# An S5, gMLP and expert-mixture inference step: small rows loaded whole, earlier chunk loads, half tables, POOL rotations, eight-row weight runs

## The chip, the cores and the metric

The kernel runs on one NeuronCore of a Trainium2 chip. The core has TensorE (PE, matrix products; its weight loads are listed as PEld), VectorE (DVE), ScalarE (ACT), GpSimd (POOL) and SyncE (SP), which here only issues DMAs. Each engine works through its own instructions in the order in which they were written and waits on semaphores. The metric is the device time of one execution in microseconds; lower is better.

## The reference

One decoder layer over 2048 prompt tokens and 8 sequences of 8 sample tokens, model width 1024. Head group A is a gated MLP that mixes positions within chunks of 128. Head group B is a diagonal complex state-space layer (S5): 32 groups of 16 channels with 64 complex states each, then GELU and GLU. A mixture of 32 experts (top 2) follows.

```python
ada = jax.nn.silu(c) @ w_ada + b_ada
h = modulate(x, g_norm1, sh1, sc1)
proj = h @ w_in                      # 1024 -> 3 x 512
u = jax.nn.gelu(proj[..., :D_A]); v = head_layer_norm(gelu(proj[..., D_A:2 * D_A]), ln_g, ln_b)
s_in = proj[..., 2 * D_A:]
a_out = u * chunk_spatial_mix(v, w_s, b_s)
# S5: h_t = (ar + i ai) h_{t-1} + (br + i bi) u_t, ar + i ai = exp((lam_re + i lam_im) exp(log_dt))
y = C_re h_re - C_im h_im + d_skip * u
b_out = gelu(y) * sigmoid(gelu(y) @ w_glu + b_glu)
x = x + gt1 * (jnp.concatenate([a_out, b_out]) @ w_out)
h = modulate(x, g_norm2, sh2, sc2)
x = x + gt2 * hier_moe(h, ...)       # h = silu(xb @ w1[e]) * (xb @ w3[e]); h @ w2[e]
```

Outputs are the final normed rows, the S5 states and the sample rows of v. All is float32; a product is made of three matmuls on high and low parts ("hi" and "lo").

## The kernel before

Five stages follow each other, each a block of its own with one written program per engine: `front` (L283), `s5` (L1186), `mixout` (L1517), `route` and `experts` (L1922, L2175) and `final`. In the trace the front lies from 0 to 488 us, the recurrence (`s5`) to 688, mixout to about 1045, the expert stage from 1107 to about 1620.

The front takes the 17 token tiles in six groups of three or two (`FRONT`). Group 0 is special: SP loads the vectors and w_ada (L446 to L475), PE makes the modulation row (L755), DVE adds its bias (L980), and w_in is loaded in 12 pieces by POOL and split into high and low parts by ACT (`win_s` and `uv`) and DVE (`low_piece`). For each group PE computes the s part, then v, then u (`rows_step`); before each u step it turns a piece of the next group's x (L773), which ACT copies with the gain and DVE splits (`low`, L963). DVE has, beside that, to build the S5 tables: `powers`, `factors`, `rotations` (18 complex products, L1022 to L1037, `cmul` at L905 to L909) and for each of 16 pairs of groups `pair(p)` (L1039 on), of which POOL stores 1536 columns as `s5_tables` (L593 to L604) and the toeplitz rows. DVE runs `rotations()` between two u steps of group 0. POOL, after the w_in pieces, stores the sample blocks of w_s (L577), then rows of the bias (L580), then a zero pad for the toeplitz rows (L587); DVE's first pair waits for the pad.

The recurrence works on chunks of 8 tokens. SP loads in a written order (L1246 on): 16 chunk rows, 8 sample groups of 64-byte pieces, two tables, the initial states, 8 toeplitz loads, then two more tables; in each batch of two pairs it loads the next two tables as soon as both outputs are computed, and stores y. ACT and DVE regroup the chunk rows by group of channels, PE turns them (`fill`) into uT. Then for a batch b, PE runs `additions(b + 2)` (the terms that enter the states, L1349), DVE the scan over chunks (`batch(b)`, ends with L1479), and PE the two `outputs` (L1365 to L1372). In between DVE makes the low parts of w_glu and w_out (`low(n)`, L1446).

```python
                for b in range(NBATCH):
                    outputs(2 * b)
                    outputs(2 * b + 1)
                    if b + 2 < NBATCH:
                        additions(b + 2)
```

Mixout loads y (12 DMAs for the first group, L1607), multiplies with the GLU weight (L1685), waits with the sigmoid `z` (L1774) for `small_ld`, which counts the router's small loads too, and adds the output product (L1708 to L1710). Meanwhile POOL writes zeros over the blocks of `expert_rows` that may stay empty (L1668), eight of them at once and the others as tiles are done. The expert stage gathers rows (xg), turns them by 128 columns (L2342), splits them, and multiplies with the weights of each expert; `hid` is turned at L2374.

## Time and profile before

| | us |
|---|---|
| median of 3 runs | 1751.36 (1748.81 to 1752.66) |
| the profiled execution | 1746.57 |
| its span on the core | 1744.8 |
| granted TensorE clock, mean | 0.869 of 2.4 GHz |

| engine | busy us | share | instructions |
|---|---|---|---|
| PE | 1323.8 | 76% | 6756 |
| PEld | 1051.4 | 60% | 6757 |
| DVE | 960.4 | 55% | 2307 |
| ACT | 588.1 | 34% | 979 |
| POOL | 392.1 | 22% | 400 |

The page also divides the span into 40 slices of 43.6 us. A digit is the busy share in tenths:

```profile
PE   1686999998926663399899982799999999999100
DVE  1368646656324342154466658586555476565398
PEclk9698999999966776699999985599999999999655
DMA  5634354351277543655446210799877599795686
```

The slices 12 to 16 are the recurrence, slice 24 is the routing. DMAs moved 338.55 MB. A DMA share can exceed 1 in the windows.

### The profile page before, as it was taken

The page shows a single profiled execution, that of the slowest core. Times are in us where ns is not written, and L with a number is a line of the kernel's source. Part 1 is how long each engine was busy: PE and PEld are TensorE (multiplying, and loading weights), DVE is VectorE, ACT ScalarE, POOL GpSimd, SP SyncE. Part 2 cuts the span into 40 slices and gives each one's busy share as a digit, 9 for nine tenths or more (in the row PEclk, how much of TensorE's full clock was granted, in tenths as well). Part 3 has the DMA queues.
Part 4 walks back from the last instruction along what each step waited for, and adds up shares of the span by engine and source line. Part 5 has one row for each costly group of instructions (what it writes and reads, how often), then busy time and mean ns, then how long its engine had stood idle before and what let it go on. Part 6 is the DMA issues. An engine that isn't in the chain of part 4 may idle for free. (4 is left out here: it accounts for less than half of the span.)

```text
span 1744.8 us, 25676 instructions
## 1 busy us (share of the span) xinstructions
PE 1323.8 (76%) x6756; PEld 1051.4 (60%) x6757; DVE 960.4 (55%) x2307; ACT 588.1 (34%) x979; POOL 392.1 (22%) x400
## 2 busy tenths in 40 slices
PE   1686999998926663399899982799999999999100
PEld 0464777776725552378788871587778877778000
DVE  1368646656324342154466658586555476565398
ACT  2352425233211111121122110276545476565111
POOL 0011202112100001000010000256442356364331
PEclk9698999999966776699999985599999999999655
DMA  5634354351277543655446210799877599795686
GB/s 190 203 101 124 107 175 165 123 164 57 71 193 151 156 146 81 188 159 161 157 156 194 103 61 29 248 311 382 312 248 252 181 358 388 266 363 199 250 327 258
DMA packets 184993, 338.55 MB, mean 194 GB/s; under 512 B 31545, under 2 KB 119689, under 8 KB 183890
## 3 DMA queue, kind: packets, MB, share of 16 engines
q1 hardware_dynamic: 159538, 250.92, 43.5%
q0 software_dynamic: 25376, 86.66, 14.8%
q8 instruction: 40, 0.66, 0.2%
q14 instruction: 39, 0.32, 0.1%
HBM read 242.98 MB, written 94.40 MB: 193 GB/s over the span
## 5 line engine op out<-in xcount | busy, mean ns | idle before, releaser
L2312 POOL TENSOR_TENSOR down_lo<-expert_raw,down_hi (+1 forms) x64 | 153.5, 2420 | 201.5 <-ACT down_hi L2406 201.5
L2456 DVE TENSOR_TENSOR up_lo<-expert_raw,up_hi (+1 forms) x128 | 160.7, 1315 | 19.2 <-ACT up_hi L2401 16.4
L256 PE MATMUL ps_up<-up_hi,xT_hi 128*128 x400 | 162.0, 405 | 6.1 <-DVE up_lo L2456 2.9
L257 PE MATMUL ps_up<-up_lo,xT_hi 128*128 x400 | 157.2, 393 | 0.0
L258 PE MATMUL ps_up<-up_hi,xT_lo 128*128 x400 | 156.9, 392 | 0.0
L2401 ACT ACTIVATE up_hi<-expert_raw (+1 forms) x128 | 125.3, 1060 | 1.6 <-issue 0.5
L1708 PE MATMUL ps_out<-wout_hi,catT 128*128 128x512 f32 (+1 forms) x272 | 108.4, 399 | 0.0
L1710 PE MATMUL ps_out<-wout_hi,catT 128*128 128x512 f32 (+1 forms) x272 | 106.8, 393 | 0.0
L1709 PE MATMUL ps_out<-wout_lo,catT 128*128 128x512 f32 (+1 forms) x272 | 106.8, 392 | 0.0
L256 PEld LDWEIGHTS ps_up<-up_hi,xT_hi 128*128 128x128 f32 x400 | 75.8, 189 | 26.3 <-issue 11.9
L258 PEld LDWEIGHTS ps_up<-up_hi,xT_lo 128*128 128x128 f32 x400 | 75.8, 189 | 16.4
L257 PEld LDWEIGHTS ps_up<-up_lo,xT_hi 128*128 128x128 f32 x400 | 75.9, 190 | 14.3
L1668 POOL DMA_DIRECT2D expert_rows<-blank x31 | 26.8, 986 | 250.2 <-DVE x L1857 245.8
L2394 ACT ACTIVATE xT_hi<-ps_xT 128x512 fp32r<-128x512 f32 x102 | 55.4, 599 | 70.1 <-PE ps_xT L2342 69.5
L2450 DVE TENSOR_TENSOR xT_lo<-ps_xT,xT_hi 128x512 fp32r<-128x512 f32 x102 | 65.7, 686 | 22.3 <-ACT xT_hi L2394 21.8
L258 PE MATMUL ps_y<-down_hi,hidT_lo 128*128 x196 | 77.6, 396 | 0.0
L256 PE MATMUL ps_y<-down_hi,hidT_hi 128*128 x196 | 77.5, 396 | 0.0
L257 PE MATMUL ps_y<-down_lo,hidT_hi 128*128 x196 | 77.5, 396 | 0.0
L2406 ACT ACTIVATE down_hi<-expert_raw (+1 forms) x64 | 64.3, 1053 | 32.6 <-issue 28.1
L2306 POOL DMA_INDIRECT xg<-moe_in_rows,idx x54 | 59.4, 1100 | 43.2 <-POOL idx L2303 42.4
L2473 DVE TENSOR_SCALAR yo<-ps_y,gcol 128x512 f32<-128x512 f32 x49 | 36.7, 748 | 55.3 <-PE ps_y L258 54.1
L1795 ACT ACTIVATE h<-x 128x1024 f32<-128x1024 f32 (+1 forms) x17 | 18.0, 1061 | 144.5 <-DVE x L1857 144.5
(407 smaller groups left out, 3115.2 us busy)
## 6 DMA issues: line engine op xcount, KB each, us to landing
expert_raw<-in_w SPq DMA_DIRECT2D x96, 1024.0 KB
expert_rows<-yo SPq DMA_DIRECT2D x49, 512.0 KB
x<-in_x_prompt SPq DMA_DIRECT2D x32, 512.0 KB, 4.8
stage<-in_w_ada SPq DMA_DIRECT2D x32, 512.0 KB, 4.3
expert_rows<-blank POOLq DMA_DIRECT2D x31, 512.0 KB, 5.6
tab<-s_tables SPq DMA_DIRECT2D x16, 768.0 KB, 5.4
wada_early<-in_w_ada SPq DMA_DIRECT2D x8, 1024.0 KB, 15.4
s_tables<-pair_scratch POOLq DMA_DIRECT2D x32, 256.0 KB, 2.6
```

The costliest lines, as they stand in the source:

```text
L256: pe.matmul(out, left(0, k), right(0, k), start=k == 0, stop=False)
L257: pe.matmul(out, left(0, k), right(1, k), start=False, stop=False)
L258: last = pe.matmul(out, left(1, k), right(0, k), start=False, stop=k == n - 1)
L1708: pe.matmul(out, cat[:, 0, k, spot(m)], S.wout_hi[:, k, cols], start=k == 0, stop=False)
L1709: pe.matmul(out, cat[:, 0, k, spot(m)], S.wout_lo[:, k, cols], start=False, stop=False)
L1710: last = pe.matmul(out, cat[:, 1, k, spot(m)], S.wout_hi[:, k, cols], start=False, stop=k == KD - 1)
L2306: pool.indirect_dma_start(out=xg[:, par, :], out_offset=None, in_=S.h2_d, in_offset=bass.IndirectOffsetOnAxis(ap=idx[:, par:par + 1], axis ...
L2312: pool.tensor_tensor(down_piece(down_lo, run, m), raw_piece(run, 2, m, 1), down_piece(down_hi, run, m).bitcast(F32), ALU.subtract).then_in ...
L2401: act.activation(up_piece(up_hi, run, m), raw_piece(run, m // 2, m % 2, KD // 2), ACT.Copy).then_inc(up_h, 1)
L2406: act.activation(down_piece(down_hi, run, m), raw_piece(run, 2, m, 1), ACT.Copy).then_inc(down_h, 1)
L2450: dve.tensor_tensor(xT_lo[:, par, ks, :], pX[:, h, :].rearrange("p (k t) -> p k t", k=4), xT_hi[:, par, ks, :].bitcast(F32), ALU.subtract) ...
L2456: dve.tensor_tensor(up_piece(up_lo, run, m), raw_piece(run, m // 2, m % 2, KD // 2), up_piece(up_hi, run, m).bitcast(F32), ALU.subtract).t ...
```

## The change

1. In the front's start, `dt`, the first norm's gain and the gMLP bias are each loaded as whole rows, and the last two are turned by PE beside the lambdas. In the SBUF plan, `win_s` moves ahead of the early w_ada area.
2. The 18 complex products of the rotations run on POOL with a tile set of their own; DVE's pair 0 waits for them before it uses the rotations.
3. The chunk rows are loaded by SP in the front's last group and regrouped there (first half of the channels) by ACT.
4. In the recurrence a table comes as two halves, one that the additions and the scan need (`state_tables`) and one for the outputs (`output_tables`). The sample rows are one load, regrouped by POOL and ACT. The router's small loads are issued there. POOL makes the low parts of the weights. Additions stand between the two outputs of a batch.
5. In mixout, half of the first y loads are issued by ACT, and every blank block waits for a finished tile.
6. Expert weights are read with 8 (w1, w3) or 2 (w2) neighbouring rows per partition, and xg and hid are turned by columns that lie 8 or 2 apart.

```diff
-        ldt = a.log_dt[0:1, :].rearrange("o (a g) -> o g a", g=2)
-        for g in range(2):
-            sp.dma_start(dt[g * ST:(g + 1) * ST, :], ldt[:, g, :].to_broadcast([ST, PAIRS])).then_inc(lam_ld, 16)
+        sp.dma_start(dt[:, :], a.log_dt[0:1, :].to_broadcast([P, G])).then_inc(lam_ld, 16)
+        sp.dma_start(g1row, a.g_norm1.rearrange("o (k p) -> (o k) p", p=P)).then_inc(lam_ld, 16)
+        sp.dma_start(bsrow, a.b_s[0]).then_inc(lam_ld, 16)
...
-                sp.dma_start(g1col[:, :], a.g_norm1.rearrange("o (k p) -> p (o k)", p=P)).then_inc(brow_ld, 16)
...
+        sp.wait_ge(s_out, 16 * NT)
+        sp.wait_ge(s_mm, NT)
+        rows = S.s_d[0:SEQ, :].rearrange("(c s) n -> s c n", s=Q)
+        for kt in range(2):
+            for m in range(8):
+                sp.dma_start(S.chunk[:, 8 * kt + m, :], rows[8 * kt + 7 - m]).then_inc(S.chunk_ld[kt], 16)
...
+        def tmul(o_re, o_im, x_re, x_im, y_re, y_im, t):
+            turns.did(pool.tensor_tensor(o_re, x_re, y_re, ALU.mult))
+            turns.did(pool.tensor_tensor(o_im, x_re, y_im, ALU.mult))
+            turns.link(pool.tensor_tensor(t, x_im, y_im, ALU.mult))
+            turns.link(pool.tensor_tensor(o_re, o_re, t, ALU.subtract))
+            turns.link(pool.tensor_tensor(t, x_im, y_re, ALU.mult))
+            turns.link(pool.tensor_tensor(o_im, o_im, t, ALU.add))
+
+        def rotations():
+            own = [t[:, :] for t in turn_c]
+            (cr, ci), (er, ei) = (tmp[5][:, :], tmp[3][:, :]), own[0:2]
+            spare = own[2:4]
+            pool.wait_ge(pw_ok, 1)
+            for i in range(4):
+                tmul(er, ei, cr, ci, cr, ci, own[4])
+                (cr, ci), (er, ei) = (er, ei), spare if i == 0 else (cr, ci)
+            for t, top in ((rB, 16), (rA, 8)):
+                turns.did(pool.memset(t[:, 0, :, 0:1], 1.0))
+                turns.link(pool.memset(t[:, 1, :, 0:1], 0.0))
+                n = 1
+                while n < top:
+                    sh = [P, PAIRS, n]
+                    tmul(t[:, 0, :, n:2 * n], t[:, 1, :, n:2 * n], t[:, 0, :, 0:n], t[:, 1, :, 0:n], fan(cr, sh), fan(ci, sh),
+                         turn_t[:, :, 0:n])
+                    tmul(er, ei, cr, ci, cr, ci, own[4])
+                    (cr, ci), (er, ei) = (er, ei), (cr, ci)
+                    n *= 2
+            pool.sem_inc(turn_ok, 1)
...
+        rotations()
...
+            if g == NF - 1:
+                act.wait_ge(v_mm, NT)
+                for kt in range(2):
+                    act.wait_ge(S.chunk_ld[kt], 16 * 8)
+                    act.activation(*by_group(S, kt, 0), ACT.Copy).then_inc(S.grouped_a, 1)
...
+            if p == 0:
+                dve.wait_ge(turn_ok, 1)
...
+        def load_tx(p):
+            sp.dma_start(tx[:, p % NB, :], S.tab_d[p][:, 0:HALF]).then_inc(tx_ld[p % NB], 16)
+
+        def load_ty(p):
+            sp.dma_start(ty[:, p % NB, :], S.tab_d[p][:, HALF:TABW]).then_inc(ty_ld[p % NB], 16)
+
+        sp.dma_start(work[0:NSEQ, 0:DSEQ * DA].rearrange("q (t n) -> q t n", t=DSEQ),
+                     S.s_d[SEQ:TOK, :].rearrange("(q t) n -> q t n", t=DSEQ)).then_inc(ss_ld, 16)
         for i, t in enumerate((a.state_ssm_re, a.state_ssm_im)):
             sp.dma_start(h0_in[:, i, :], t[0].rearrange("q (a g) p -> (q a) (g p)", g=2)).then_inc(h0_ld, 16)
+        for p in range(NB):
+            load_tx(p)
         for m in range(8):
             s = 7 - m
             sp.dma_start(toep[m * GC:(m + 1) * GC, :, :], S.kpad_d[:, :, P - s * GC:2 * P - s * GC]).then_inc(toep_ld, 16)
-        for p in range(2, 4):
-            load_tab(p)
+        for p in range(NB):
+            load_ty(p)
+        sp.dma_start(S.bglu[:, :], a.b_glu.rearrange("o (j p) -> p (o j)", p=P)).then_inc(S.small_ld, 16)
+        sp.dma_start(S.wr[:, :, 0:EG], a.w_group[0].rearrange("(k p) n -> p k n", p=P)).then_inc(S.small_ld, 16)
+        sp.dma_start(S.wr[:, :, EG:NR], a.w_expert[0].rearrange("(k p) n -> p k n", p=P)).then_inc(S.small_ld, 16)
+        sp.dma_start(S.br[:, 0:EG], a.b_group.to_broadcast([P, EG])).then_inc(S.small_ld, 16)
+        sp.dma_start(S.br[:, EG:NR], a.b_expert.to_broadcast([P, NE])).then_inc(S.small_ld, 16)
...
+            if 2 * b + NB < PAIRS:
+                sp.wait_ge(h_ok, 2 * b + 2)
+                for p in (2 * b, 2 * b + 1):
+                    load_tx(p + NB)
+                for p in (2 * b, 2 * b + 1):
+                    sp.wait_ge(y_mm, 2 * p + 2)
+                    load_ty(p + NB)
...
+        pool.tensor_copy(*samples(0)).then_inc(ss_ok, 1)
         for n in range(10):
-            if n >= 2:
-                pool.wait_ge(w_l, n - 1)
-            pool.dma_start(raw_part(n), part(w_glu, w_out, n)).then_inc(raw_ld[n % 2], 16)
+            pool.wait_ge(w_h, n + 1)
+            pool.tensor_tensor(part(S.wglu_lo, S.wout_lo, n), raw_part(n), part(S.wglu_hi, S.wout_hi, n).bitcast(F32),
+                               ALU.subtract).then_inc(w_l, 1)
+            if n + 2 < 10:
+                pool.wait_ge(w_l, n + 1)
+                load(n + 2)
...
         for b in range(NBATCH):
             outputs(2 * b)
-            outputs(2 * b + 1)
             if b + 2 < NBATCH:
                 additions(b + 2)
-
-        pe.wait_ge(fin_ok, 2)
-        pe.wait_ge(x_free, NBATCH)
-        for i in range(2):
-            pe.transpose(pX[0:PAIRS, 0, 0, i * P:(i + 1) * P], h[:, :, i, CH], ident[:, :])
-        for i in range(2):
-            last = pe.transpose(pX[:, 1, 0, i * P:(i + 1) * P], fin[:, i, :, :].rearrange("p q a -> p (q a)"), ident[:, :])
-        last.then_inc(f_mm, 1)
+            if b == NBATCH - 1:
+                finals()
+            outputs(2 * b + 1)
...
-            if n >= FULL + 8:
-                pool.wait_ge(x2_ok, (n - FULL - 8) // 2 + 1)
+            pool.wait_ge(x2_ok, (n - FULL) // 2 + 1)
...
+        for n, i in enumerate(GROUPS[0]):
+            for k in range(2, 4):
+                act.dma_start(yf[:, k, n * P:(n + 1) * P], y_rows(i, k)).then_inc(y_ld2, 16)
+        act.wait_ge(y_ld2, 32 * len(GROUPS[0]))
...
-    return [(t[0].rearrange("e (k p) n -> e p k n", p=P), k) for t, k in ((a.w1, KD), (a.w3, KD), (a.w2, DE // P))]
+    return [(t[0].rearrange("e (p k) n -> e p k n", p=P), k) for t, k in ((a.w1, KD), (a.w3, KD), (a.w2, DE // P))]
...
-                last = pe.transpose(pX[:, k // 4, k % 4 * P:(k % 4 + 1) * P], xg[:, q, k * P:(k + 1) * P], ident[:, :])
+                last = pe.transpose(pX[:, k // 4, k % 4 * P:(k % 4 + 1) * P], xg[:, q, :].rearrange("p (c k) -> p k c", k=KD)[:, k, :], ident[:, :])
...
-                last = pe.transpose(pT[:, k * P:(k + 1) * P], hid[:, k * P:(k + 1) * P], ident[:, :])
+                last = pe.transpose(pT[:, k * P:(k + 1) * P], hid[:, :].rearrange("p (c k) -> p k c", k=KH)[:, k, :], ident[:, :])
```

**Where instructions stand.** SP in the recurrence's start before (`tab` is a whole table; L1248 the chunk rows):

```order
L1248 DMA chunk_rows<-s_in 128x512 x16
L1256 DMA sample_groups<-s_in 8x32x16 x8
L1253 DMA tab<-s_tables 128x1536 x2
L1261 DMA h_in<-in_state_ssm_re 128x128
L1261 DMA h_in<-in_state_ssm_im 128x128
L1264 DMA toep<-toeplitz_rows 16x32x128 x8
L1253 DMA tab<-s_tables 128x1536 x4
L1273 DMA s_out<-ys 128x4x128 x2
```

and now (`wr`, `bglu`, `br` are the router's and the GLU's small loads):

```order
L1300 DMA s_work<-s_in 8x4096
L1303 DMA h_in<-in_state_ssm_re 128x128
L1303 DMA h_in<-in_state_ssm_im 128x128
L1295 DMA state_tables<-s_tables 128x768 x4
L1308 DMA toep<-toeplitz_rows 16x32x128 x8
L1298 DMA output_tables<-s_tables 128x768 x4
L1311 DMA bglu<-in_b_glu 128x4x1
L1312 DMA wr<-in_w_group 128x8x4
L1313 DMA wr<-in_w_expert 128x8x32
L1314 DMA br<-in_b_group 128x4
L1315 DMA br<-in_b_expert 128x32
L1295 DMA state_tables<-s_tables 128x768 x2
```

The chunk rows left for the front, and the small loads stand ahead of the first tables that are loaded again. POOL in the front, after the w_in pieces, before (`spatial_bias_sample` is the bias rows, `toeplitz_rows` the zero pad):

```order
L577 DMA ws_samp<-ws 8x4x8 x8
L580 DMA spatial_bias_sample<-spatial_bias 8x512 x8
L586 MEMSET pair_scratch 16x128
L587 DMA toeplitz_rows<-pair_scratch 512x1x128
L588 TENSOR_TENSOR pair_scratch<-ident,dd 16x512
```

and now, with the start and the end of the rotations (18 products of six instructions, and four MEMSETs):

```order
L627 DMA ws_samp<-ws 8x4x8 x8
L590 TENSOR_TENSOR turn_c<-tmp 128x16
L591 TENSOR_TENSOR turn_c<-tmp 128x16
L592 TENSOR_TENSOR turn_c<-tmp 128x16
L593 TENSOR_TENSOR turn_c<-turn_c 128x16
L594 TENSOR_TENSOR turn_c<-tmp 128x16
...
L595 TENSOR_TENSOR turn_c<-turn_c 128x16
L631 DMA spatial_bias_sample<-spatial_bias 8x512 x8
L637 MEMSET pair_scratch 16x128
L638 DMA toeplitz_rows<-pair_scratch 512x1x128
```

The bias rows and the pad now stand behind the rotations. PE in a batch of the recurrence, before (`ps_s` are outputs, `ps_state` additions):

```order
L1372 MATMUL ps_s<-h,tab 128x128 x4
L1365 MATMUL ps_s<-uT,toep 128x136 x2
L1372 MATMUL ps_s<-h,tab 128x136 x4
...
L1372 MATMUL ps_s<-h,tab 128x128 x4
L1349 MATMUL ps_state<-uT,tab 64x136 x2
L1349 MATMUL ps_state<-uT,tab 64x128 x2
```

and now:

```order
L1435 MATMUL ps_s<-h,output_tables 128x128 x4
L1411 MATMUL ps_state<-uT,state_tables 64x136 x2
L1411 MATMUL ps_state<-uT,state_tables 64x128 x2
...
L1411 MATMUL ps_state<-uT,state_tables 64x128 x2
L1428 MATMUL ps_s<-uT,toep 128x136 x2
L1435 MATMUL ps_s<-h,output_tables 128x136 x4
```

The additions moved from behind the second output of a batch to between the two.

## Rows read from the trace of the kernel before

**Rows 1.** Windows: stretch, length; PE, PEld, DVE, ACT, POOL busy; clock; DMA share; GB/s

```profile
5.00:25.00 20.00, 0.32 (x3) 0.22 (x3) 0.23 (x1) 0.48 (x1) 0.00 (x0) 1.00 0.17 47
25.00:55.00 30.00, 13.27 (x62) 1.88 (x66) 8.75 (x34) 8.41 (x15) 1.45 (x2) 0.74 1.00 381
520.00:535.00 15.00, 10.09 (x100) 9.62 (x100) 8.23 (x16) 5.21 (x10) 1.11 (x2) 0.84 1.28 114
545.00:678.00 133.00, 84.23 (x642) 69.12 (x640) 49.29 (x133) 18.64 (x45) 3.19 (x6) 0.74 0.40 123
1150.00:1600.00 450.00, 436.66 (x2084) 352.24 (x2083) 277.76 (x389) 276.89 (x402) 217.58 (x148) 1.00 0.86 304
```

**Rows 2.** Timeline of the start: begin, length, engine, line, operation, [idle before]

```profile
26.70 0.22 ACT L615 ACTIVATE tmp<-dt 128x16 f32<-128x16 f32 x1 [21.22 <-DMA dt<-in_log_dt]
57.93 0.68 DVE L980 TENSOR_TENSOR u<-ps_a,u 128x512 f32<-128x512 f32 x1
```

**Rows 3.** Timeline 100 to 206 us; then one wait, DMA and group row

```profile
105.45 4.41 POOL L577 DMA_DIRECT2D ws_samp<-ws  x8 [0.29 <-POOL ws L571]
...
152.69 1.09 PE L896 MATMUL ps_x<-ident,pair_scratch 128*128 128x128 f32 x4 [14.64 <-ACT rs_col L730]
...
169.78 0.42 DVE L1061 TENSOR_TENSOR pair_scratch<-pw_re,bb 128x256 f32<-128x256 f32 x1
...
198.13 0.49 PE L773 MATMUL ps_t<-ident,x 128*128 128x128 f32 x3
...
200.82 0.55 DVE L963 TENSOR_TENSOR hT<-h,hT 128x384 fp32r<-128x384 f32 x1
...
201.42 0.49 PE L773 MATMUL ps_t<-ident,x 128*128 128x128 f32 x3
...
203.56 0.32 POOL L601 TENSOR_TENSOR pair_scratch<-pair_scratch 16x32 f32<-16x32 f32 x1 [5.81 <-ACT pair_scratch L672]
...
DVE stats L1098 <- ACT v L680: 12.3, 3, 4.5
...
toeplitz_rows<-pair_scratch POOLq DMA_DIRECT2D x1, 256.0 KB, 6.0
...
L2303 POOL COPY idx<-slot_tok 128x1 int32 (+1 forms) x54 | 33.1, 613 | 72.6 <-POOLq L1977 61.0 <-PE ps_xT L2342 10.7 <-issue 0.5
```

**Rows 4.** Timeline of the recurrence

```profile
502.54 1.91 ACT L1408 ACTIVATE chunk_groups<-chunk_rows 128x2048 f32<-128x2048 f32 x1 [21.86 <-DMA chunk_rows<-s_in]
...
559.99 2.03 PE L1349 MATMUL ps_state<-uT,tab 128*64 128x136 f32 x16 [3.69 <-DMA tab<-s_tables]
...
581.38 1.28 PE L1365 MATMUL ps_s<-uT,toep 128*128 128x136 f32 x4 [1.84 <-DVE h L1479]
...
650.49 1.28 PE L1365 MATMUL ps_s<-uT,toep 128*128 128x136 f32 x4 [1.79 <-DVE h L1479]
...
676.96 0.71 PE L1372 MATMUL ps_s<-h,tab 64*128 64x128 f32 x8
```

**Rows 5.** Timeline of the way into mixout

```profile
688.27 17.65 SPq L1607 DMA_DIRECT2D yf<-s_out  x12
...
711.47 1.77 ACT L1763 ACTIVATE yT<-yf 128x384 fp32r<-128x384 f32 x4 [31.86 <-DMA yf<-s_out]
...
726.44 1.05 ACT L1774 ACTIVATE z<-ps_z,bglu 128x384 f32<-128x384 f32 x2 [8.38 <-DMA br<-in_b_expert]
...
738.45 0.48 PE L1708 MATMUL ps_out<-wout_hi,catT 128*128 128x512 f32 x1
```

**Rows 6.** Weight loads by form: least, median, largest ns; last, mean ns

```profile
L2342 PEld LDWEIGHTS ps_xT<-ident,xg x408: 138/141/230, 1113.3 to 1609.5; 128*128 128x128 f32 x136
...
L1390 PEld LDWEIGHTS ps_state<-ident,h x2: 93/98/103, 682.9 to 683.0; 128*16 128x16 f32 x2
...
L1392 PEld LDWEIGHTS ps_state<-ident,fin x2: 226/226/226, 683.1 to 683.3; 128*128 128x128 f32 x2
...
L755 PEld LDWEIGHTS ps_a<-wada_early,cT 128*32 128x32 f32 x64 | 1.6, 136 | 26.0 <-DMA wada_early<-in_w_ada 23.7 <-DVE tmp L928 2.2
```

More of the change, by code:

```diff
@@ L190, in build @@
         S.blocks_out, S.pad_out = (ctx.enter_context(nc.semaphore(n)) for n in ("ws_blocks", "pad_stored"))
+        S.chunk_ld = [ctx.enter_context(nc.semaphore(f"chunk_loaded{i}")) for i in range(2)]
+        S.grouped_a, S.small_ld = (ctx.enter_context(nc.semaphore(n)) for n in ("groups_act", "router_loaded"))
+        S.logits = sb(ctx, "logits", [P, NT, NR])
+        with ExitStack() as start:
+            S.chunk = sb(start, "chunk_rows", [P, Q, DA])
+            S.turn = sb(start, "chunk_groups", [P, 2, G, 8 * GC])
         names, used = ExitStack(), []
@@ L195, in build @@
         assert [t.num for t in used] == list(S.spent)
-        S.logits = sb(ctx, "logits", [P, NT, NR])
         with ExitStack() as mid:
-            with ExitStack() as start:
-                S.turn = sb(start, "chunk_groups", [P, 2, G, 8 * GC])
             S.wout_hi = sb(mid, "wout_hi", [P, KD, D], F32R)
-            with ExitStack() as start:
-                S.chunk = sb(start, "chunk_rows", [P, Q, DA])
             S.wout_lo = sb(mid, "wout_lo", [P, KD, D], F32R)
@@ L275, in first_token, with by_group @@
     return GROUPS[g][0] * P
+def by_group(S, kt, half):
+    gs = slice(half * G // 2, (half + 1) * G // 2)
+    src = S.chunk[:, 8 * kt:8 * kt + 8, half * DA // 2:(half + 1) * DA // 2].rearrange("p m (g o) -> p g m o", o=GC)
+    return S.turn[:, kt, gs, :].rearrange("p g (m o) -> p g m o", o=GC), src
 FRONT = ((0, 1, 2), (3, 4, 5), (6, 7, 8), (9, 10, 11), (12, 13, 14), (15, TP))
@@ L287, in front @@
         W = TPG * P
+        win_s = sb(st, "win_s", [P, 2, KD, DA], F32R)
         with ExitStack() as early:
@@ L327, in front @@
         li = sb(st, "li", [P, PAIRS])
-        dt = sb(st, "dt", [P, PAIRS])
+        dt = sb(st, "dt", [P, G])
+        turn_c = [sb(st, f"turn_c{i}", [P, PAIRS]) for i in range(5)]
+        turn_t = sb(st, "turn_tmp", [P, PAIRS, 8])
         tmp = [sb(st, f"tmp{i}", [P, PAIRS]) for i in range(8)]
@@ L613, in _ @@
                 st_.did(act.activation(c9, c9, ACT.Silu))
-                act.wait_ge(lam_ld, 64)
-                st_.link(act.activation(tmp[7][:, :], dt[:, :], ACT.Exp))
+                act.wait_ge(lam_ld, 80)
+                by_pair = dt[:, :].rearrange("p (a g) -> p g a", g=2)
+                act.activation(tmp[7][0:ST, :], by_pair[0:ST, 0, :], ACT.Exp)
+                st_.link(act.activation(tmp[7][ST:P, :], by_pair[ST:P, 1, :], ACT.Exp))
                 act.wait_ge(dv, 2)
@@ L919, in _ @@
                 c.did(dve.tensor_copy(lr[:, :], pT[:, 0:PAIRS]))
+                c.did(dve.tensor_copy(g1col[:, :], pT[:, 2 * PAIRS:2 * PAIRS + KD]))
+                c.did(dve.tensor_copy(bs_col[:, :], pT[:, 2 * PAIRS + KD:2 * PAIRS + KD + HEADS]))
                 c.link(dve.tensor_copy(li[:, :], pT[:, PAIRS:2 * PAIRS]))
@@ L1168, in _ @@
                             factors()
-                        if g == 0 and k == 4:
-                            rotations()
                         if k < 5 or g == NF - 1:
@@ L1207, in s5 @@
         ident = S.ident
-        c_ld = [sem(f"chunk_loaded{i}") for i in range(2)]
-        p_a, p_d, ss_ld, f_mm0, e_a, e_d, ys_ok, ys_out = (sem(n) for n in (
-            "groups_act", "groups_dve", "sample_loaded", "turned_mm", "uT_copied_act", "uT_copied_dve", "y_sample_copied", "y_sample_stored"))
-        tab_ld = [sem(f"tables_loaded{i}") for i in range(NB)]
+        p_d, ss_ld, ss_ok, f_mm0, e_a, e_d, ys_ok, ys_out = (sem(n) for n in (
+            "groups_dve", "sample_loaded", "sample_grouped", "turned_mm", "uT_copied_act", "uT_copied_dve", "y_sample_copied",
+            "y_sample_stored"))
+        tx_ld, ty_ld = ([sem(f"{n}_tables_loaded{i}") for i in range(NB)] for n in ("state", "output"))
         raw_ld = S.weights_ld
@@ L1228, in raw_part, with samples @@
             return raw[:, n % 2, :].rearrange("p (k n) -> p k n", k=2) if n < 2 else raw[:, n % 2, :]
-        def by_group(kt, half):
+        def samples(half):
             gs = slice(half * G // 2, (half + 1) * G // 2)
-            src = S.chunk[:, 8 * kt:8 * kt + 8, half * DA // 2:(half + 1) * DA // 2].rearrange("p m (g o) -> p g m o", o=GC)
-            return S.turn[:, kt, gs, :].rearrange("p g (m o) -> p g m o", o=GC), src
+            src = srow[:, ::-1, gs, :].rearrange("q t g h -> q g t h")
+            return S.samp[:, gs, :].rearrange("q g (m h) -> q g m h", m=DSEQ), src
         def evacuated(n):
@@ L1370, in outputs @@
                                 r = slice(g * ST, (g + 1) * ST)
[L1371 to L1372 removed]
+                                m0 = 256 + 256 * i + 128 * half
+                                last = pe.matmul(pY[:, banks[g], at:at + width], ty[r, p % NB, m0:m0 + P], h[r, p, i, lo:CH],
                                                  start=False, stop=i == 1)
@@ L1438, in _ @@
                         hi(b + 2)
+                act.wait_ge(ys_ok, NBATCH)
+                for m in range(8):
+                    act.dma_start(S.ys_d.rearrange("(g o) t q -> t o g q", o=GC)[m], ysamp[m * GC:(m + 1) * GC, :, :]).then_inc(ys_out, 16)
             @block.vector
@@ L1600, in load_y @@
                     for n, i in enumerate(GROUPS[g]):
-                        for k in range(4):
+                        for k in range(4 if g else 2):
                             if i == TP:
```

188 lines of the change are left out of this document (80 added, 108 removed).

## The prediction

> **What bounds the kernel now.** I read four views in this order. The first page's busy digits in 40 slices show that TensorE (PE) works nearly all the time in three long stages (front, mixout, experts) and that holes lie at the start, near 150 us, in the recurrence and between recurrence and mixout. The windows put numbers on the holes [rows 1]: 0.32 us of PE work in the 20 us from 5, 84 of 133 us in the recurrence. The experts are full (437 of 450 us), so only something that lengthens PE's own work can matter there. The timelines then show what ends each hole: transfers at the start [rows 2], VectorE (DVE) near 150 [rows 3], transfers and DVE in turn in the recurrence [rows 4], transfers again into mixout [rows 5]. Last, rows by form give the price of a weight load [rows 6]. The profiled execution took 1746.57 us; the runs' median is 4.8 us above it. I sum against the former and carry the gain over unchanged.
>
> **Start: small rows loaded whole: -17.** From 5 to 25 us the core moved 47 GB/s at a DMA share of 0.17, and 381 GB/s from 25 to 55 [rows 1]: the queues were behind pieces of 4 bytes. dt, two broadcasts of 64 x 16 such pieces (2048), was awaited for 21.22 us by the Exp at 26.70 [rows 2]; g1col adds 1024 and bs_col 512. All become rows of 128 to 512 bytes. The eight w_ada pieces (8.4 MB), x (1.6), the bias rows (0.3) and the first w_in pieces (about 2.1) are some 12 MB, at the later rate 32 us; from 4 us on that is about 36 us. The gate for all that follows is DVE's add at 57.93, behind w_ada and a w_in piece; that piece I put at 39 and the add at 41: 17 us earlier. Everything up to the recurrence hangs on this add. Bounds: 14 (a third of the old stall stays) to 20 (the whole low stretch).
>
> **Rotations from DVE to GpSimd (POOL): -12.** PE waited 14.64 us until 152.69, while DVE computed 18 complex products [rows 3]; a hole also leaves a low clock behind it (the mean is 0.74 in the recurrence's window, 1.00 in the experts'), which I estimate at 2 us here: 16.6 gross. POOL has no row for this shape. Nearest: 0.32 us for 16x32, and 0.29 us of waiting after another POOL instruction (at 105.45). A product is six instructions with four such hops: 6 x 0.32 + 4 x 0.29 = 3.1, times 18 = 56 us. The bounds are 44 (two hops hidden) and 92 (0.61 us a small instruction, as in the mean of POOL's idx copies, plus hops). POOL starts at 110 in the old count, ends at 166, issues eight DMAs (4.4 us, as the eight at 105.45) and the pad store, which lands 6.0 later: 177. DVE's pair(0) waits for that store; it would otherwise start at 169.78 - 16.6 = 153. After it DVE owes, before the first low of the next group's hT, its work between 169.78 and 200.82: 31.0 less waits of 12.3 = 18.7. So that low comes at 195.7, against 200.82 - 16.6 = 184.2. PE can work two turns ahead (3.3 us each, 198.13 to 201.42), so of these 11.5 it stands about 4.6. Net -12. Up to some 51 us on POOL nothing stands; at 92 the stall is 40 and the edit costs 21: bounds -16.6 and +21, my value lies by the nearest row. That the pair tables come later I price at nothing: PE's steps in the front don't wait for them, and the last of them is stored well within the groups that follow.
>
> The Trainium skill ("SBUF — State Buffer", section "SBUF: two separate sides") has POOL and DVE lock one shared port pair when DVE reads two SBUF inputs. The rotations then delay DVE's two-input work and it them. No row here has this pairing at this size; by the rule POOL's 56 us would grow by the share of DVE's busy time, towards 75, the stall with it.
>
> **Chunk rows in the last group: +0.6.** ACT groups its halves before the last group's GELUs, 2 x 1.91 us less its idle time there. In exchange the recurrence starts without this load.
>
> **Recurrence: -36.** (a) Its first work waited for chunk rows until 502.54 [rows 4]; loaded early, PE can start 15 us sooner. (b) But what then gates is the tables. The eight toeplitz loads are 4096 pieces of 512 bytes, 2.1 MB at the 114 GB/s seen then [rows 1]: 18.5 us, done about 517.5; four output tables, 522.5; then five small router loads, some 2800 pieces of 4 to 16 bytes. Before, with 2304 such pieces in the queue behind y, their reader went at 726.44, 15 us after y's at 711.47 [rows 5]; so about 14 us here, since they start at an empty queue, and the state tables for batch 2, queued behind them, land near 542. additions(2), at 559.99 before after a wait for its tables, begins about 543: -17. (c) Periods were (650.49 - 581.38)/4 = 17.3 us, with PE waiting 1.8 for DVE's h in each. The table of the next batch no longer waits for both outputs, DVE no longer splits weights, and additions stand between the two outputs: I take 15.5 (13 if only PE's work of 84/133 of the time remains plus one hop; 17 if DVE's scan still sets it): -7 over four. (d) At the end the two last batches (the last outputs began at 676.96, 26.5 after the row at 650.49) need about 8 each: -10. (e) The ys stores leave SP: -2. Together -36, bounds 22 (tables at 556, period 17) and 52 (at 533, 13). The ten splits go to POOL, busy for 3.2 of 133 us there; without that cover, mixout's first product would wait for the last.
>
> **Into mixout: -27.5.** Before, y landed at 711.47, 23 us after the stage began: twelve loads by SP beside 4 MB of blank rows. Then ACT's z waited 8.38 more, until 726.44, for the router's small loads [rows 5]; project(0) began at 738.45. Now the loads are shared by two engines, no blanks run beside, and the small ones are done. y after about 6.5 us, the GLU in the 12 us from 726.44 to 738.45, 4 us of turning and copying before: 22.7 after the stage's start at 688.3 where it was 50.2. Bounds 20 and 30. The blanks go to later stages, where POOL idles; 4 MB at 381 GB/s are 11 us of a queue that is used to 0.4 to 0.9, and cost nothing as long as PE is not waiting for transfers.
>
> **Experts: -1.** Weights come in runs of 8 KB in place of 1 to 4 KB, at 304 GB/s and a share of 0.86; but PE idles only 13 of 450 us, so little can be had. The price is that 408 transposes of xg read columns 32 bytes apart and 100 of hid 8 bytes apart. The load of xg takes 141 ns now [rows 6]. A load of 16 columns from h at a stride of over 1 KB took 98 ns; by contiguous ones of 32 columns (136) and 128 (226 at the low clock) 16 columns would take about 121. So a stride shows no price here. Bounds: -3 and +35 (below).
>
> **Sum.** -17 - 12 + 0.6 - 36 - 27.5 - 1 = -93: the profile at 1653.6, the median at 1658.
>
> **The rivals.**
> B: the recurrence stays gated and the rotations are long. For it: DVE's scan ended PE's wait each period; POOL's price is not measured. Recurrence -22, rotations -2: gain about 68, time 1684.
> C: the queue clears fast. If the small loads are spread over the 16 engines beside the tables, these land at 533, the period is 13, and the shorter holes leave the clock high (0.74 in the recurrence's window, 1.00 in the experts'). Start 20, rotations 15, recurrence 48, mixout 30: gain 117, time 1634. Against it: the 15 us behind the old small loads.
> D: the strided weight load runs at half its rate. Then 141 ns become the low clock's 226: +85 ns on 408 loads, +35: 1693. If the load reads the wrong side of the pair (moving), the same price falls on the 98 ns row, which does not show it.
> The Trainium skill ("SBUF — State Buffer", "Specifications (TRN2)") says that a 16-byte line wants at least two hits for full bandwidth; xg at 32 bytes has one per line. That speaks against the change; the row of h disagrees with it, at 16 columns only.
> E, the other side: the same mechanism, far dearer. PE is full in this stage, so nothing hides it: from 93/408 = 0.23 us more per transpose the whole gain is gone, and at 0.25 the time is about 1760. That is nearly three times the present load.
>
> **How the numbers follow.** A result within 0.2% of before (3.5 us, about what the runs can tell apart) would need several of these to cancel. Chances: the forecast 0.50 (1640 to 1680), C 0.17, B 0.15, D 0.12, E and anything like it 0.06. The range 1626 to 1700 takes in B, C and most of D. Faster 0.93, same 0.02, slower 0.05.
>
> **What would show it.** Start: no wait for dt, DVE's first add near 41 us. Rotations: POOL busy for about 35 of 56 us in a run of L590 to L595 rows, and a PE wait before group 1's u steps of about 5 us; none means that POOL was faster. Recurrence: the first PE wait for state tables near 540, behind the small loads' landing; if it ends before 535, C. Mixout: project(0) about 23 us after the stage's first y load. Experts: the load for ps_xT at 141 ns; over 200 means D or E. The forecast is wrong if the recurrence and the way into mixout together give under 45 us or over 85.

## The result, and the profile after

| | before | after |
|---|---|---|
| median of 4 runs, us | 1750.09 | 1634.01 (1632.02 to 1638.78) |
| ratio to before | | 0.935 (0.9333 to 0.9368) |
| span of the profiled execution, us | 1744.8 | 1630.3 |
| granted TensorE clock, mean | 0.869 | 0.892 |

The forecast was 1658, with its own range from 1640 to 1680 and 1626 to 1700 in all; what came lies 24 us below it, at the time that rival C had. The gain of 116 us divides by stage as follows (times in us from the start of the span). Each line takes an event of both traces; the differences are between one execution of each, and in the kernels here that share its front PE's first turn of the recurrence begins between 453.65 and 456.23 us. The additions of batch 2 (`additions`, the terms that enter the states) ran in two halves before, at 555.18 and 559.99; the row takes the second, as the prediction did, and from the first the step would be 4.8 us less.

| event | before | after | moved | this step | forecast |
|---|---|---|---|---|---|
| DVE's first add (u from ps_a) | 57.93 | 39.54 | -18.4 | -18.4 | -17 |
| SP's first load of the recurrence | 489.94 | 456.52 | -33.4 | -15.0 | -11.4 |
| additions of batch 2 | 559.99 | 500.29 | -59.7 | -26.3 | -17 |
| last output's products | 676.96 | 590.73 | -86.2 | -26.5 | -17 |
| first y load of mixout | 688.27 | 600.20 | -88.1 | -1.8 | -2 |
| first product of project(0) | 738.45 | 626.93 | -111.5 | -23.4 | -27.5 |
| first turn of xg | 1113.33 | 1004.01 | -109.3 | +2.2 | 0 |
| last turn of hid | 1618.04 | 1504.86 | -113.2 | -3.9 | -1 |
| end of the span | 1744.8 | 1630.3 | -114.5 | -1.3 | 0 |

Windows of the start, after, with the columns of [rows 1]: the quiet 20 us are gone, and the 30 us after them are no longer full.

```profile
5.00:25.00 20.00, 8.65 (x40) 1.56 (x39) 5.42 (x33) 8.19 (x16) 0.00 (x0) 1.00 0.99 398
25.00:55.00 30.00, 15.53 (x63) 6.65 (x64) 11.15 (x19) 11.23 (x18) 2.89 (x4) 0.70 0.52 187
```

The timeline of the start, after, answers [rows 2]: dt's reader at 7.85, not 26.70, and the add at 39.54.

```profile
7.85 0.21 ACT L668 ACTIVATE tmp<-dt 64x16 f32<-64x16 f32 x1
...
39.54 0.68 DVE L1043 TENSOR_TENSOR u<-ps_a,u 128x512 f32<-128x512 f32 x1
```

The timeline of the rotations, after, answers [rows 3]: the first product on POOL, the last instruction, the DMAs behind it, and DVE's wait.

```profile
90.16 0.23 POOL L590 TENSOR_TENSOR turn_c<-tmp 128x16 f32<-128x16 f32 x1
90.33 0.23 POOL L591 TENSOR_TENSOR turn_c<-tmp 128x16 f32<-128x16 f32 x1
90.51 0.22 POOL L592 TENSOR_TENSOR turn_c<-tmp 128x16 f32<-128x16 f32 x1
90.81 0.22 POOL L593 TENSOR_TENSOR turn_c<-turn_c 128x16 f32<-128x16 f32 x1
91.11 0.22 POOL L594 TENSOR_TENSOR turn_c<-tmp 128x16 f32<-128x16 f32 x1
91.41 0.24 POOL L595 TENSOR_TENSOR turn_c<-turn_c 128x16 f32<-128x16 f32 x1
91.73 0.22 POOL L590 TENSOR_TENSOR turn_c<-turn_c 128x16 f32<-128x16 f32 x1
...
128.16 0.22 POOL L595 TENSOR_TENSOR turn_c<-turn_c 128x16 f32<-128x16 f32 x1
129.03 4.60 POOL L631 DMA_DIRECT2D spatial_bias_sample<-spatial_bias  x8 [0.65 <-POOL turn_c L595]
...
139.45 0.43 DVE L1107 TENSOR_TENSOR pair_scratch<-pw_re,bb 128x256 f32<-128x256 f32 x1 [5.25 <-DMA toeplitz_rows<-pair_scratch]
```

A product of 16 columns takes 1.57 us (90.16 to 91.73), not 3.1; those that fill the tables have up to 128 columns, and all 18 take 38 us, not 56. DVE waits 5.25 us for the pad. PE's only wait between 100 and 200 us is 0.88 us, for a weight of the modulation; the old one of 14.64 is gone.

PE's three longest waits from 440 to 640 us, after (us in total, times, longest). The first two are the recurrence's, the third is mixout's:

```profile
PE ps_state L1411 <- DMA state_tables<-s_tables: 25.2, 6, 5.2
PE ps_s L1428 <- DMA output_tables<-s_tables: 14.8, 1, 14.8
PE ps_aT L1746 <- DMA a_rows<-gmlp_rows: 11.5, 1, 11.5
```

From batch 2 on the additions wait 3.6 to 5.2 us for their state tables in each batch. One period of the recurrence's timeline, after, shows why (it answers the rows at 581.38 and 650.49 of [rows 4]):

```profile
514.40 3.43 PE L1411 MATMUL ps_state<-uT,state_tables 128*64 128x136 f32 x32 [3.95 <-DMA state_tables<-s_tables]
517.76 0.94 PE L1428 MATMUL ps_s<-uT,toep 128*128 128x136 f32 x4
...
521.15 0.32 SPq L1298 DMA_DIRECT2D output_tables<-s_tables  x1
521.85 0.92 SPq L1322 DMA_DIRECT2D s_out<-s_work  x2
...
522.82 1.20 SPq L1295 DMA_DIRECT2D state_tables<-s_tables  x2
523.12 2.40 POOL L1357 TENSOR_TENSOR wout_lo<-weights_raw,wout_hi 128x1024 fp32r<-128x1024 f32 x1 [10.51 <-ACT wout_hi L1465]
523.36 2.45 DVE L1538 TENSOR_TENSOR h<-s_work 128x256 f32<-128x256 f32 x1
...
528.20 3.57 PE L1411 MATMUL ps_state<-uT,state_tables 128*64 128x136 f32 x32 [4.03 <-DMA state_tables<-s_tables]
```

SP issues the next state tables at 522.82, behind a load of output tables at 521.15 and its store of y at 521.85. The load waits for the second outputs and the store for their GELU, and PE runs the second outputs behind the additions of 514.40. From 528.20 back: 5.4 us of landing, 1 us of stores, 0.7 of GELU, 3.4 of outputs, 3.4 of additions. It is a circle of 13.8 us through the order in which SP and PE were written. The store and its GELU are about 1.7 us of it; without them the wait for the second outputs, at the output tables, would hold the next state tables all the same. A second thing stands out: DVE's subtraction takes 2.45 us beside POOL's split, where the same instruction took 0.42 before the change.

### The profile page after: what moved, and what is told of

It is laid out like the page before. It is cut to its first block and busy times, and to the rows that moved or that the text cites. A ratio compares the mean times of both kernels' runs of the same rounds, so it can differ in the third digit from the quotient of the medians.

```text
span 1630.3 us, 25699 instructions
## 1 busy us (share of the span) xinstructions
PE 1313.5 (81%) x6758; PEld 1046.3 (64%) x6759; DVE 942.7 (58%) x2187; ACT 589.4 (36%) x981; POOL 452.2 (28%) x523
```

## The experiments

Each changes one thing in the changed kernel, the later ones in its successor as told. The kernel before was run on the same chip each time, its medians between 1746.8 and 1749.9; a difference in us is that of the ratios times 1750, against 0.935. The changed kernel's own interval is 3 us to each side, so a difference under about 5 us is not told apart from none: this holds for low_dve, small_in_mixout, plain_turns and old_layout. Those of chunk_in_s5 and blanks_now are just clear of it.

| kernel | median | ratio (95%) | against the changed one, us |
|---|---|---|---|
| sp_order | 1600.99 | 0.9153 (0.9137 to 0.9169) | -34 |
| low_dve | 1634.89 | 0.9358 (0.9334 to 0.9382) | +1 |
| sp_order_low_dve | 1611.22 | 0.9210 (0.9195 to 0.9226) | -25 |
| pe_order | 1596.67 | 0.9137 (0.9119 to 0.9155) | -37 |
| rot_dve | 1650.62 | 0.9432 (0.9416 to 0.9447) | +14 |
| dt_pieces | 1652.30 | 0.9444 (0.9428 to 0.9459) | +16 |
| chunk_in_s5 | 1641.49 | 0.9382 (0.9357 to 0.9406) | +6 |
| small_in_mixout | 1639.27 | 0.9368 (0.9353 to 0.9384) | +3 |
| blanks_now | 1642.04 | 0.9391 (0.9366 to 0.9416) | +7 |
| plain_turns | 1631.98 | 0.9345 (0.9322 to 0.9368) | -1 |
| old_layout | 1632.88 | 0.9351 (0.9312 to 0.9391) | 0 |
| toep_two_queues | 1597.98 | 0.9140 (0.9118 to 0.9162) | -37 |

**sp_order.** SP issues the next state tables ahead of the output tables and the store.

```diff
-                for b in range(NBATCH):
+                def next_tx(b):
                     if 2 * b + NB < PAIRS:
                         sp.wait_ge(h_ok, 2 * b + 2)
                         for p in (2 * b, 2 * b + 1):
                             load_tx(p + NB)
+
+                next_tx(0)
+                for b in range(NBATCH):
+                    next_tx(b + 1)
+                    if 2 * b + NB < PAIRS:
                         for p in (2 * b, 2 * b + 1):
                             sp.wait_ge(y_mm, 2 * p + 2)
...
```

> Changed kernel, but SP issues the state tables of batch b+3 ahead of the output tables of batch b+2 and of the y store of batch b. Theory loop: the 14.4 us from one additions to the next are a circle through SP's written order (additions 3.4, second outputs 3.3, GELU and y store about 2, then the table is issued and lands 5.4 later). With the table issued at h, the period falls to PE's own work, 10 to 11 us, and 5 periods give 17 to 22 us: about 1614 us. Rival scan: h itself is late (DVE's last subtraction takes 2.45 us beside POOL's split), the issue moves little, and the time stays above 1626 us.

The gain is larger than either theory had it. PE's timeline in sp_order:

```profile
503.00 3.51 PE L1416 MATMUL ps_state<-uT,state_tables 128*64 128x136 f32 x32 [3.50 <-DMA state_tables<-s_tables]
512.56 2.02 PE L1416 MATMUL ps_state<-uT,state_tables 128*64 128x136 f32 x32
520.63 2.02 PE L1416 MATMUL ps_state<-uT,state_tables 128*64 128x136 f32 x32
```

The period is 8.07 us (512.56 to 520.63), not 10 to 11. I had added PE's work from rows behind a wait, at the low clock. The windows of one additions each, first two of the changed kernel and then one of sp_order, with the columns of [rows 1] (the granted clock is the number ahead of the DMA share; 0.50 is 1.2 GHz, 1.00 is 2.4):

```profile
500.30:504.00 3.70, 3.70 (x32) 3.37 (x32) 0.00 (x0) 0.00 (x0) 0.00 (x0) 0.50 0.27 107
514.40:517.76 3.36, 3.35 (x32) 3.03 (x32) 0.00 (x0) 0.00 (x0) 0.00 (x0) 0.56 0.63 253
...
512.56:514.58 2.02, 2.02 (x35) 1.85 (x33) 2.02 (x2) 0.67 (x2) 1.72 (x2) 1.00 0.69 206
```

The additions take 2.8 to 3.8 us behind their waits, at granted clocks of 0.50 to 0.71, and 2.02 us at 1.00 once PE has no holes. The waits cost twice, by themselves and by the clock.

**low_dve.** The splits on DVE, one behind each batch; POOL only loads.

```diff
-                    pool.tensor_tensor(part(S.wglu_lo, S.wout_lo, n), raw_part(n), ...)
+                    dve.tensor_tensor(part(S.wglu_lo, S.wout_lo, n), raw_part(n), ...)   # low(n), behind batch(n - 1)
```

> Changed kernel, but DVE makes the low parts of w_glu and w_out in the recurrence (one after each batch) and POOL only loads. Theory loop: DVE is not in the circle; the 128x256 subtraction falls from 2.45 to about 0.42 us, but additions start when they did: 1631 to 1636 us. Rival scan: h 2 us earlier in each of 8 batches, less 1.2 for the split when it is in the way: 1620 to 1626 us.

The time is 1634.89, in the theory's range: DVE is not in the circle. The subtraction is short there (0.42 us in all eight batches), and the last additions still begin at 572.08, against 572.15 in the changed kernel.

**sp_order_low_dve.** Both. 

> Both edits together. Theory loop: PE's own work is the bound once the table is early, so this is within 3 us of the kernel with SP's order alone, 1610 to 1617 us. Rival scan: only here, with h early and the table early, does the period fall; 8 us or more below the better of the two single edits.

Neither theory: it is 10 us slower than sp_order alone. The median lies in the first range, 1610 to 1617, but that range stood around a sp_order of 1614, so this is luck. Once PE is the bound, DVE's order matters again: PE waits for h three times, up to 3.25 us (at 562.51), where in sp_order it never does after its first outputs. The row of the split, by line (busy, mean ns, idle before it):

```profile
L1566 DVE TENSOR_TENSOR wout_lo<-weights_raw,wout_hi 128x1024 fp32r<-128x1024 f32 x8 | 9.8, 1225 | 42.3 <-ACT wout_hi L1466 42.3
```

The split waits 42.3 us in all for ACT, and the next batch's scan stands behind it (how much of the 42.3 DVE would have idled anyway is not shown). POOL is the better place here, in spite of the collision.

**pe_order.** PE's old order in the recurrence.

```diff
                     outputs(2 * b)
-                    if b + 2 < NBATCH:
-                        additions(b + 2)
                     if b == NBATCH - 1:
                         finals()
                     outputs(2 * b + 1)
+                    if b + 2 < NBATCH:
+                        additions(b + 2)
```

> Changed kernel, but PE computes both outputs of a batch and then the additions of batch b+2, as before the change. Theory loop: the store of y no longer stands behind the additions, the table lands beside the second outputs, period 10 to 11 us: about 1614 us, as with SP's order; so putting the additions in the middle cost what the half tables could have given. Rival, as in my forecast: the additions in the middle keep DVE fed, and taking them back costs 1 to 2 us a period: 1642 to 1650 us.

The circle opens from the other side, with the same result and a little more: the additions of batch 2 (499.48) have no wait either, where sp_order's waited 3.50. The forecast of this run, 1614, had the same error as sp_order's, PE's work at the low clock. A window over five periods, PE, PEld, DVE, ACT, POOL busy as in [rows 1]:

```profile
499.00:540.00 41.00, 40.98 (x450) 34.92 (x452) 30.92 (x89) 12.61 (x30) 14.56 (x10) 1.00 0.96 317
```

PE is full at the full clock. So additions between the outputs, which I had counted as a gain, cost 37 us with SP's order as it is. No kernel here is faster than this one, 9% below the one before.

**rot_dve.** The 18 products back on DVE between two u steps of group 0.

```diff
+                        if g == 0 and k == 4:
+                            turn_on_dve()       # as rotations() before
...
-                rotations()                     # on POOL
...
-                    if p == 0:
-                        dve.wait_ge(turn_ok, 1)
```

> Changed kernel with the 18 products of the rotations back on DVE, between two u steps of group 0. Theory: on POOL they cost nothing (PE has no wait there, DVE's pad wait of 5.2 us hides), so all of the old hole comes back: 1649 to 1652 us, with a PE wait of about 14.6 us. Rival: other work had shrunk that hole by now, under 8 us come back: below 1642 us.

All of it comes back (1650.62, in the theory's range), with the old hole in PE's timeline:

```profile
133.16 1.09 PE L955 MATMUL ps_x<-ident,pair_scratch 128*128 128x128 f32 x4 [14.61 <-ACT rs_col L782]
```

**dt_pieces.** Only dt in 4-byte pieces again.

```diff
-                sp.dma_start(dt[:, :], a.log_dt[0:1, :].to_broadcast([P, G])).then_inc(lam_ld, 16)
+                for g in range(2):
+                    sp.dma_start(dt[g * ST:(g + 1) * ST, 0:PAIRS], ldt[:, g, :].to_broadcast([ST, PAIRS])).then_inc(lam_ld, 16)
```

> Changed kernel, but dt is loaded again as two broadcasts of 64x16 pieces of 4 bytes (2048 pieces); the gain and bias rows stay whole. Theory: dt's pieces at the head of the queues made the quiet 20 us, so 14 to 18 of the 18.4 us come back: 1648 to 1652 us. Rival: g1col's 1024 pieces did as much, in proportion 2048 of 3584: about 10 us, 1644 us.

These 2048 pieces alone bring back the whole stall. The windows of its start, and its add:

```profile
5.00:25.00 20.00, 0.52 (x5) 0.42 (x4) 0.23 (x1) 0.68 (x1) 0.00 (x0) 1.00 0.16 44
25.00:55.00 30.00, 13.56 (x64) 2.09 (x68) 8.89 (x36) 8.38 (x15) 1.44 (x2) 0.69 0.99 380
...
58.02 0.68 DVE L1043 TENSOR_TENSOR u<-ps_a,u 128x512 f32<-128x512 f32 x1
```

58.02 against 57.93 before: g1col in pieces had cost nothing that shows here. SP issued it only at 28.23 us, behind the quiet stretch, and bs_col later still.

**chunk_in_s5.** The 16 chunk loads and ACT's grouping at the recurrence's start. 

> Changed kernel with the chunk rows loaded and grouped by ACT at the recurrence's start, as before. Theory queue: the first outputs wait for toeplitz and output tables, whose 512-byte pieces hold the queue; the 16 loads in front push these by 9 us and PE's fill has slack of 15 us, so about 9 to 12 us are lost: 1643 to 1646 us. Rival: the full 15 us of the fill's start are lost, 1649 us or more.

PE's first turns begin 15.3 us later, its first outputs 11.3 later, and these wait for h, no longer for tables. The last additions are 9.7 us later (581.86 against 572.15), as the theory had it. By the ratios about 6 us are lost (1 to 10), and the median is a little under its range:

```profile
471.53 3.67 PE L1375 MATMUL ps_state<-ident,chunk_groups 128*128 128x128 f32 x16 [23.10 <-ACT chunk_groups L1469]
...
502.38 1.24 PE L1423 MATMUL ps_s<-uT,toep 128*128 128x136 f32 x4 [7.27 <-DVE h L1537]
```

**small_in_mixout.** The five small loads behind the first y loads again. 

> Changed kernel with the router's five small loads back in mixout, behind the first y loads. Theory: in the recurrence they cost little (3.6 us wait for tables at 500 us), and in mixout z waits for them as before (8.4 us and the low clock after it): net 5 to 8 us slower, 1639 to 1642 us. Rival of my forecast: they hold the first state tables by 12 us or more in the recurrence, so moving them out gains there what it costs later: 1630 to 1636 us.

```profile
602.48 1.76 ACT L1813 ACTIVATE yT<-yf 128x384 fp32r<-128x384 f32 x4 [16.13 <-DMA yf<-s_out]
...
617.31 1.05 ACT L1824 ACTIVATE z<-ps_z,bglu 128x384 f32<-128x384 f32 x2 [8.61 <-DMA br<-in_b_expert]
```

The old wait returns in z (8.61 us), and the recurrence gives part of it back: its last additions begin 111.5 us behind its first turn (453.65 to 565.13), 4.4 less than in the changed kernel (456.23 to 572.15). By the ratios 3 us stay, by the medians 5; the theory's range has the one and not the other.

**blanks_now.** Eight blank blocks written at mixout's start. 

> Changed kernel, but POOL writes eight blank blocks (4 MB) at mixout's start, as before. Theory: they share the transfers with y, which lands 5 us or more later than its 9.7 us: 1639 to 1644 us. Rival: y was late for SP's issue of twelve loads, which two engines now share, and the blanks only fill free time: 1632 to 1637 us.

The theory holds, 1642.04 in its range: y's first reader waits 28.20 us, 11.7 more than the 16.48 of the changed kernel, so the blanks don't only fill free time:

```profile
621.82 1.76 ACT L1815 ACTIVATE yT<-yf 128x384 fp32r<-128x384 f32 x4 [28.20 <-DMA yf<-s_out]
```

**plain_turns** reads xg and hid by contiguous columns; **old_layout** has the old weight layout as well.

```diff
-    xg[:, q, :].rearrange("p (c k) -> p k c", k=KD)[:, k, :]
+    xg[:, q, k * P:(k + 1) * P]
...
-    hid[:, :].rearrange("p (c k) -> p k c", k=KH)[:, k, :]
+    hid[:, k * P:(k + 1) * P]
```

> Changed kernel with contiguous columns in the turns of xg and hid, the weight layout kept (so the experts' result is not the reference's). Theory: the strided weight load is slower (193 against 141 ns) but runs beside the moving columns: eight turns take 1.06 us against 1.04, so at most 1 to 2 us are gained: 1632 to 1634 us. Rival: 52 ns on 508 loads are exposed, 26 us gained: 1608 us.

> Changed kernel with the weights' old layout (runs of 4 and 1 KB) and contiguous turns. Theory: the longer runs gave 3 to 5 us in the experts' stage (its first to last turn 492.4 us against 496.2), so 1636 to 1639 us. Rival: the layout did nothing, that difference is chance: 1632 to 1635 us, as with plain turns.

The turns' loads by form (least, median, largest ns), changed kernel:

```profile
L2397 PEld LDWEIGHTS ps_xT<-ident,xg x408: 185/193/231, 1004.0 to 1496.4; 128*128 128x128 f32 x136
```

plain turns:

```profile
L2397 PEld LDWEIGHTS ps_xT<-ident,xg x408: 137/141/230, 1001.1 to 1493.2; 128*128 128x128 f32 x136
```

The stride does have a price, 52 ns a load, but the 408 matmuls beside it are busy for 57.6 us with it and 55.6 without: 2 us are exposed, and 1.7 on the 100 turns of hid (21.7 against 20.0). The layout's gain is not settled by the runs: old_layout's median, 1632.88, lies in the rival's range, with an interval of 7 us to each side. The traces say more. The span from the first xg turn to the last hid turn is 504.7 us before and 503.6 in old_layout, 500.9 after and 500.6 in plain_turns, and between 500.5 and 502.8 in the ten other kernels, which all have the new layout: about 3 us for the longer runs.

**toep_two_queues** is pe_order, with four of the eight toeplitz loads issued by ACT. 

> The kernel with PE's old order in the recurrence, and ACT issues four of the eight toeplitz loads. Theory queue: the loads of 512-byte pieces are held by one engine's queue (SP's issue of eight takes 16 us), two queues run side by side, and the first outputs start 5 to 8 us earlier: 1589 to 1592 us. Rival transfers: the pieces themselves fill the transfer engines (share 1.28 in that window before), so nothing is gained, and ACT's copies come later by the issue: 1596 to 1602 us.

The wait for output tables falls from 16.7 to 8.1 us, but PE's earlier work is pushed back by the ACT queue's issue and by h_in, which lands later, so the first outputs gain 2.7 us (488.11 against 490.79); the additions of batch 2 then wait 3.52 for tables and start at 499.51, where pe_order has 499.48:

```profile
465.44 0.69 PE L1387 MATMUL ps_s<-ident,h_in 128*128 128x128 f32 x2 [4.12 <-DMA h_in<-in_state_ssm_im]
...
488.11 1.24 PE L1428 MATMUL ps_s<-uT,toep 128*128 128x136 f32 x4 [8.12 <-DMA output_tables<-s_tables]
499.51 3.79 PE L1411 MATMUL ps_state<-uT,state_tables 128*64 128x136 f32 x32 [3.52 <-DMA state_tables<-s_tables]
```

The rival's range holds. From 459 us to the first outputs the DMA share is 1.12 to 1.13 in pe_order and 1.13 to 1.17 here, and SP's four toeplitz issues take 13.88 us where eight took 15.98: the second queue adds little where the transfers are full, and what is gained at one wait is lost at the next.

## Why the prediction was right, and where its sizes were off

The range held and the order of the gates held; the middle was 24 us too high, most of it in the recurrence. That the time is rival C's to the microsecond is luck: C's own terms (20, 15, 48 and 30) add up to 113 and not 117, so its time should have been 1638, and its parts came otherwise: 18.4, 15.0, 54.6 and 23.4. By the prediction's sign, recurrence and way into mixout between 45 and 85 us, they gave 78.

**Start (-17, was -18.4).** Right in mechanism and size. The pieces of dt were the whole of it, shown by dt_pieces; that g1col and bs_col shared the blame, as the text counted their pieces, falls.

**Rotations and last group (-11.4, were -15.0).** The gross gain of 16.6 was right (rot_dve, +14 by the ratio and 16.6 by the medians, with PE's wait of 14.61). The mis-sized term is POOL's price: 56 us forecast, 38 measured. I took a row of 0.32 us and added a full hop of 0.29 behind each dependent instruction; the trace has 0.22 us and 0.30 from start to start of dependent ones. At 38 us POOL stays under the 51 from which PE would stand, as the working itself said. (Two slips in it: 11.5 less two turns of 3.3 us is 4.9, not 4.6, and at 92 us of POOL the edit would have cost about 24, not 21.) The stretch to 75 us did not come, but the collision behind it is in the trace, one instruction at a time: a POOL instruction whose like takes 0.22 us took 1.26 beside one of DVE with two SBUF inputs.

```profile
93.97 1.22 DVE L1007 TENSOR_TENSOR uv<-stage,uv 128x1024 fp32r<-128x1024 f32 x1
94.01 1.26 POOL L593 TENSOR_TENSOR turn_c<-turn_c 128x16 f32<-128x16 f32 x1
```

About 18 of the 112 instructions are longer than their like, the others of them at 0.38 to 0.80 us. Taken from the shortest distance between the same two instructions, an estimate is 7 of the 38 us; that each of them met DVE is not shown.

**Recurrence up to batch 2 (-17, was -26.3).** The order of gates was right: toeplitz, output tables (14.8 us of waiting), state tables behind the small loads. The output tables came when forecast (first outputs at 491.06, or 524.5 in the count of the old trace, against 522.5). The mis-sized term is the small loads: 14 us behind the output tables' landing. SP's issue of the five did take 16 us (479.82 to 495.77), but 11 of them passed while those tables were still landing, and PE had the first outputs to do in the rest; its wait behind them was 3.61 us. (Not all their pieces are of 4 to 16 bytes, as the text said; 1152 of some 2800 have 128.) small_in_mixout confirms the size: there the additions of batch 2 don't wait. The additions then begin at 533.7 in the old count, which is C's 533, though with C's reason, small loads spread beside the tables, tested only this far. In chunk_in_s5 the additions of batch 2 begin 11.8 us later (512.07), so that much of the step is the chunk rows. The single sample load, in place of eight whose issue took 10.88 us ahead of the tables, has not been tested by itself, nor have the half tables.

**The rest of the recurrence (-17, was -26.5).** The forecast had the period at 15.5, with PE still held by DVE's h; it was 14.4 and bound by something that I had not seen, the circle of SP's waits for the second outputs and PE's additions. The trace before had already shown that tables held PE longer than h, in each period, and the text named h alone:

```profile
590.76 1.12 PE L1349 MATMUL ps_state<-uT,tab 128*64 128x136 f32 x16 [1.26 <-DMA tab<-s_tables]
595.15 1.42 PE L1349 MATMUL ps_state<-uT,tab 128*64 128x136 f32 x16 [3.27 <-DMA tab<-s_tables]
598.88 1.27 PE L1365 MATMUL ps_s<-uT,toep 128*128 128x136 f32 x4 [2.32 <-DVE h L1479]
...
669.11 1.27 PE L1365 MATMUL ps_s<-uT,toep 128*128 128x136 f32 x4 [9.37 <-DVE h L1479]
```

sp_order and pe_order, two independent ways to open the circle, show it; low_dve shows that DVE is not in it. Here the prediction's reason failed though its period was near, which is luck: it counted "additions stand between the two outputs" as a gain, and that very move closes the circle. Opened, the recurrence alone gives 34 to 37 us more. I had followed what the table no longer waits for, and not what is queued ahead of it in SP's order. The -26.5 are two parts. From the additions of batch 2 to those of batch 7 there are five periods, where the forecast counted four: 86.8 us before and 71.9 after, -15.0 in place of -7. From there to the last outputs it was 30.1 us (646.83 to 676.96) and is 18.6 (572.15 to 590.73), -11.5 for a forecast of -10: the 9.37 us that PE had waited for the last h, in the row at 669.11, are gone. What took that wait away is not taken apart.

**Into mixout (-27.5, were -21.2).** -23.4 up to project(0), and 2.2 us given back until routing. The mis-sized term is y's landing: its first reader went 9.7 us behind the first y load (600.20 to 609.85) where 6.5 were forecast; the rest, 17.1 us to project(0), was forecast at 16. blanks_now puts about 7 us on the blanks; for the small loads small_in_mixout has 3 us by the ratios, net of what they cost in the recurrence. The issue by two engines has not been tested by itself.

**Experts (-1, was -3.9).** Rival D's mechanism exists and its price is hidden: the load grew by 37%, the 408 turns by 2 us. The stage gained all the same, most likely by the 3 us of the longer runs. I had asked for what a load costs, where the question was whether it lies beside the matmul of the turn before. The row of h, 16 columns, misled: at 128 columns the rule of the Trainium skill ("SBUF — State Buffer", "Specifications (TRN2)", two hits per 16-byte line) agrees with the trace in direction.

## What to carry to other kernels

When a load's wait is relaxed, follow its issuing engine's queue to the instruction ahead of it: the order in which waits are written can close a circle through another engine, and neither engine looks busy (PE 70% in the changed kernel's periods). A few thousand pieces of 4 bytes at the head of the queues stall everything behind them, by 18 us here. A hole in TensorE costs its length and then the low clock after it, so the last small wait that goes may pay double: here waits of about 4 us went from each period, and it shortened by 6.3.

## What the runs showed of the hardware that was not expected

- A DVE subtraction of two 128x256 operands in SBUF took 2.45 us beside a POOL split of 2.40 us that had started 0.24 us earlier, and 0.42 us without one; it ended 0.29 us after the split. Over eight of them the median is 1.44 us. This is as the Trainium skill has it ("SBUF — State Buffer", "SBUF: two separate sides": of a DVE instruction with two SBUF inputs and a GpSimd one that reads SBUF, the loser is blocked for the whole instruction).
- Reading 128 columns 32 bytes apart as weights takes 193 ns against 141 contiguous.
- POOL started independent small instructions (128x16) 0.17 us apart and dependent ones 0.30 us apart.
- Additions of 32 matmuls took 2.02 us when PE had no hole before and 2.8 to 3.8 behind a wait of about 4 us, at granted clocks of 1.00 and of 0.50 to 0.71.
